# Six norm stages of a two-block transformer: turning rows by a product with a diagonal instead of scaling and then transposing

## The chip, the cores and the metric

The kernel is one program on one core of a Trainium2 chip. The metric is the device time of one execution in microseconds (us); lower is better. The time before is a median of 4292.33 us over 3 runs (4291.05 to 4294.51). About 0.2% of it, some 8.6 us, is what a measurement of this kernel can tell from no change.

## The reference

Two transformer blocks on 512 latent tokens ("lat") and 256 context tokens ("ctx") of width 1024. The first has three mixers (pooling, differential attention, a bidirectional linear recurrence) and a mixture of experts; the second has two layers, one with a convolution and a gated recurrence, one with latent attention, each followed by a feed-forward part. What matters here is the norm that precedes each of these parts:

```
def rms_norm(x, g):
    xf = x.astype(jnp.float32)
    y = xf * lax.rsqrt(jnp.mean(xf * xf, axis=-1, keepdims=True) + NORM_EPS)
    return (y * g.astype(jnp.float32)).astype(x.dtype)

def modulate(x, g, shift, scale):
    return rms_norm(x, g) * (1 + scale) + shift
```

Tokens of the two kinds have their own shift and scale. All is float32.

## The kernel before

The program is a row of stages. Each stage is one block in which the five engines run their own instruction lists, tied by semaphores, with a barrier of all engines at its end (helper `stage`, L48; the barrier's records stand on L57). So whatever a stage takes stands in full on the path of the whole, and nothing of the next stage's engine work begins before it ends. Only a weight tile that `bring_ahead` (L155) has asked for before the stage lands beside it.

Rows of tokens are 128x1024 tiles (partition = token, free = feature). The products that follow need them turned: partition = feature, in 8 chunks of 128 features, free = token. `normed` (L436) does norm, modulation and turning, and is called six times:

- stage 1 (`first_normed`, L837): 6 tiles, 2 ctx and 4 lat
- stage 2 (L872): 4 lat tiles before the experts; the only one whose result is one float32 tensor `hT`
- stages 3, 4 and 5 (L2104 for both layers, L2128 in layer 0): 6 tiles each
- stage 6 (L2128 in layer 1): 4 lat tiles

Except in stage 2 the result is stored as two parts, because the products on L302 work on fp32r operands in three products of parts: `parts[0]` is the result rounded to fp32r ("leading"), `parts[1]` is what rounding left over ("rest"), so that their sum is the float32 value.

How the work goes in one such stage:

- ScalarE squares each tile and sums it along the row (L459), one square after the other; VectorE divides by 1024 and adds epsilon for all tiles at once (L479); ScalarE takes the root (L461, its function table is loaded ahead of it); VectorE takes the reciprocal (L481).
- For each tile: ScalarE multiplies the rows with 1/root into `xn` (L466, two buffers); TensorE turns the 8 chunks with the transpose instruction against the identity `m.ident` (L517), four to a PSUM bank, four banks in turn; a semaphore is raised after each half tile (4 chunks).
- For each half tile VectorE reads the four chunks out of PSUM, each in an instruction of its own over 128 tokens because gain and shift are values per feature, that is per partition (L499), into `whole` (two half tiles); ScalarE rounds the half (`round_tile`, L452); VectorE subtracts to get the rest (`rest_of`, L487). VectorE's list holds the rest of the half tile before the previous one ahead of the four reads, since it frees the half of `whole` that they write.
- In stage 2 the reads on L499 write `hT` straight away and L452 and L487 don't run.

The identity product elsewhere that resembles the new one is in `gate_rows` (L412): `nc.tensor.matmul(..., wide, m.ident)`, L423, an ordinary float32 product of a 128x128 tile with a 128x128 matrix.

Of the kernel before, what the change touches and what calls it, by code (L numbers as in the profile page):

```python
# [6 lines left out]
ALU = mybir.AluOpType  # L7
# [4 lines left out]
P = 128  # L12
# [423 lines left out]
def normed(nc, m, tiles, hT, affine):  # L436
# [4 lines left out]
    kinds = sorted(affine)  # L441
    n = len(tiles)
    with ExitStack() as ctx:
        b = Memory()
        b.xn, b.sq, b.whole, b.ss, b.root, b.rstd, b.gain = buffers(nc, ctx, xn=[2, D], sq=[2, D], whole=[2, 4, P], ss=[n], root=[n], rstd=[n], gain=[len(kinds), KD])
        with stage(nc, squared=1, summed=1, rooted=1, inverse=1, scaled=1, turned=1, read=1, rounded=1, rest=1, chain=1) as (
                block, squared_sem, summed_sem, rooted_sem, inverse_sem, scaled_sem, turned_sem, read_sem, rounded_sem, rest_sem, chain_sem):
            def round_tile(act, i):

                for h in range(2):  # L450
                    act.wait_ge(read_sem, 2 * i + h + 1)
                    nc.scalar.copy(parts[0][:, 4 * h:4 * h + 4, tiles[i][1]:tiles[i][1] + P], b.whole[:, h, :, :]).then_inc(rounded_sem, 1)  # L452

            @block.scalar
            def _(act):
                for i, (x, t0, k) in enumerate(tiles):
                    if i >= 2:
                        act.wait_ge(squared_sem, i - 1)
                    nc.scalar.activation(b.sq[:, i % 2, :], x, ACT.Square, accum_out=b.ss[:, i:i + 1]).then_inc(squared_sem, 1)  # L459
                act.wait_ge(summed_sem, 1)  # L460
                nc.scalar.activation(b.root[:, :], b.ss[:, :], ACT.Sqrt).then_inc(rooted_sem, 1)  # L461
                act.wait_ge(inverse_sem, 1)
                for i in range(n):
                    if i >= 2:
                        act.wait_ge(turned_sem, 2 * (i - 1))
                    nc.scalar.activation(b.xn[:, i % 2, :], tiles[i][0], ACT.Copy, scale=b.rstd[:, i:i + 1]).then_inc(scaled_sem, 1)  # L466
                    if parts and i:
                        round_tile(act, i - 1)
                if parts:
                    round_tile(act, n - 1)  # L470

            @block.vector
            def _(dve):
# [29 lines left out]
                if parts:  # L503
                    rest_of(2 * n - 2)
                    rest_of(2 * n - 1)
# [2383 lines left out]
```

## Time and profile before

| | us |
|---|---|
| median of 3 runs | 4292.33 |
| lowest, highest | 4291.05, 4294.51 |
| the profiled execution | 4297.7 |
| its span, first to last instruction | 4295.5 |
| TensorE busy (82% of the span) | 3530.9 |
| TensorE weight loads busy (64%) | 2753.6 |
| VectorE busy (40%) | 1717.3 |
| ScalarE busy (21%) | 882.8 |
| mean granted TensorE clock | 0.908 |

The profile's page gives, for the whole span, busy time by engine, a coarse timeline, the chain of work that ended last and the costliest groups of instructions by line. The trace behind it can be asked for a timeline (instructions in order of time, neighbours merged), for stretches (busy time of each engine between two times, with the granted clock) and for groups of instructions by line and shape. Of one group the mean duration is of a single instruction; neighbouring instructions of one engine overlap a little, so that a run of them is shorter than the sum of their durations. A granted clock of 1.00 stands for 2.4 GHz, 0.50 for 1.2 GHz.

### The profile page before, as it was taken

What the parts mean: (1) busy time and instruction counts of PE and PEld (TensorE: products, weight loads), DVE (VectorE), ACT (ScalarE), POOL (GpSimd) and SP (SyncE); (2) the same over time, 40 slices, a digit from 0 to 9 for tenths busy, and PEclk for the clock granted to TensorE, in tenths of its full rate; (3) what the DMA queues carried; (4) which work ended last, traced back from release to release, by engine and by line L of the source; (5) the groups of instructions that cost most, each with busy time, mean ns of one, the idle gap of its engine ahead of it and who ended that gap; (6) DMA issues with size and microseconds to landing.
All of it is one profiled execution on the core that took longest, in us unless ns stands there. A gap on an engine that the chain in (4) does not pass through costs nothing. (4 is left out here: it accounts for less than half of the span.)

```text
span 4295.5 us, 68450 instructions
## 1 busy us (share of the span) xinstructions
PE 3530.9 (82%) x29742; PEld 2753.6 (64%) x29742; DVE 1717.3 (40%) x3137; ACT 882.8 (21%) x1426; POOL 57.0 (1%) x74
## 2 busy tenths in 40 slices
PE   4979988588986577773989976799989868979997
PEld 2858986556646333332746846688878765567887
DVE  3655544562134000004545265544420254245643
ACT  2135430042101011112011151211100112323221
POOL 0000000000000100000000000000000000000000
PEclk7979998789987799996999988899999879989998
DMA  5130006203331899993521101244421010013322
GB/s 210 60 124 4 4 10 188 84 11 111 114 112 52 326 422 424 422 422 101 155 87 54 50 2 40 68 116 112 118 91 54 0 47 25 1 35 90 97 79 79
DMA packets 379410, 494.18 MB, mean 115 GB/s; under 512 B 15994, under 2 KB 325787, under 8 KB 370436
## 3 DMA queue, kind: packets, MB, share of 16 engines
q1 hardware_dynamic: 369588, 456.12, 30.7%
q0 software_dynamic: 4432, 25.70, 1.5%
q10 hardware_dynamic: 5120, 8.39, 0.5%
q8 instruction: 215, 3.52, 0.3%
q14 instruction: 55, 0.45, 0.0%
HBM read 458.70 MB, written 31.47 MB: 114 GB/s over the span
## 5 line engine op out<-in xcount | busy, mean ns | idle before, releaser
L302 PE MATMUL banks<-leading,w_rest 128*128 128x512 f32 (+2 forms) x1920 | 699.1, 364 | 63.9 <-DVE w_rest L262 63.9
L302 PE MATMUL banks<-rest,w_leading 128*128 128x512 f32 (+2 forms) x1920 | 691.7, 360 | 0.0
L302 PE MATMUL banks<-leading,w_leading 128*128 128x512 f32 (+2 forms) x1920 | 691.1, 360 | 0.0
L302 PEld LDWEIGHTS banks<-leading,w_rest 128*128 128x128 f32 (+1 forms) x1920 | 365.1, 190 | 125.2 <-DVE w_rest L262 48.0
L302 PE MATMUL banks<-w_rest,leading 128*128 128x256 f32 (+3 forms) x1332 | 394.1, 296 | 57.0 <-DVE w_rest L262 57.0
L262 DVE TENSOR_TENSOR w_rest<-land,w_leading 128x1024 fp32r<-128x1024 f32 (+3 forms) x296 | 280.0, 988 | 357.5 <-ACT w_leading L256 357.5
L302 PEld LDWEIGHTS banks<-leading,w_leading 128*128 128x128 f32 (+1 forms) x1920 | 364.7, 190 | 59.5
L302 PEld LDWEIGHTS banks<-rest,w_leading 128*128 128x128 f32 (+1 forms) x1920 | 365.1, 190 | 57.3
L256 ACT CAST w_leading<-land 128x1024 fp32r<-128x1024 f32 (+3 forms) x296 | 239.7, 857 | 741.0 <-DMA land<-in_w_in 311.9
L302 PE MATMUL banks<-w_leading,rest 128*128 128x256 f32 (+3 forms) x1332 | 390.2, 293 | 0.0
L302 PE MATMUL banks<-w_leading,leading 128*128 128x256 f32 (+3 forms) x1332 | 389.7, 293 | 0.0
L302 PEld LDWEIGHTS banks<-w_rest,leading 128*128 128x128 f32 x1332 | 261.8, 197 | 62.3 <-DVE w_rest L262 54.0
L302 PEld LDWEIGHTS banks<-w_leading,rest 128*128 128x128 f32 x1332 | 261.7, 196 | 1.4
L302 PEld LDWEIGHTS banks<-w_leading,leading 128*128 128x128 f32 x1332 | 261.5, 196 | 1.4
L302 PE MATMUL banks<-w,fT 128*128 128x256 f32 x1056 | 230.0, 381 | 11.9 <-DMA w<-in_ffn_down 11.9
L302 PEld LDWEIGHTS banks<-w,fT 128*128 128x128 f32 x1056 | 201.9, 191 | 39.8 <-DMA w<-in_ffn_down 12.0
L1725 DVE TENSOR_TENSOR t<-banks,gate_rows 128x256 f32<-128x256 f32 x96 | 40.7, 424 | 349.4 <-PE banks L302 349.4
L1929 PE MATMUL banks<-wu,xT 128*64 128x256 f32 x1024 | 130.8, 413 | 59.9 <-DMA wu<-in_w_exp_up 59.9
L517 PE MATMUL banks<-ident,xn 128*128 128x128 f32 x256 | 59.7, 418 | 137.3 <-ACT xn L466 137.1
L348 DVE COPY side_rows<-banks 128x128 f32<-128x128 f32 x128 | 37.2, 291 | 312.7 <-PE banks L311 312.5
L1929 PEld LDWEIGHTS banks<-wu,xT 128*64 128x64 f32 x1024 | 76.9, 148 | 113.6 <-DMA wu<-in_w_exp_up 74.0
L1984 DVE TENSOR_TENSOR h<-sg,banks 128x256 f32<-128x256 f32 x32 | 13.5, 421 | 337.4 <-PE banks L1929 337.4
(532 smaller groups left out, 4803.3 us busy)
## 6 DMA issues: line engine op xcount, KB each, us to landing
wg<-in_w_exp_gate SPq DMA_DIRECT2D x32, 2048.0 KB, 28.4
wu<-in_w_exp_up SPq DMA_DIRECT2D x32, 2048.0 KB, 28.4
wd<-in_w_exp_down SPq DMA_DIRECT2D x32, 2048.0 KB, 27.9
ws<-in_ada_w SPq DMA_DIRECT2D x96, 512.0 KB, 3.9
land<-in_w_in SPq DMA_DIRECT2D x41, 1024.0 KB, 5.6
land<-in_ffn_up SPq DMA_DIRECT2D x44, 512.0 KB, 5.4
land<-in_ffn_up SPq DMA_DIRECT2D x88, 256.0 KB, 3.4
ws<-in_w_ada SPq DMA_DIRECT2D x32, 512.0 KB, 4.1
```

Of the source, the lines that this page charges most:

```text
L256: nc.scalar.copy(leading[s % 2][:, k0:k1, 0:n], slots[s % wslots][:, k0:k1, 0:n]).then_inc(rounded_sem, 1)
L262: nc.vector.tensor_tensor(rest[s % 2][:, k0:k1, 0:n], slots[s % wslots][:, k0:k1, 0:n], leading[s % 2][:, k0:k1, 0:n].bitcast(F32), ALU.su ...
L302: mm = nc.tensor.matmul(bank_of(r, kind, at), lhsT, rhs, start=(k == 0 and q == 0), stop=(k == kt - 1 and q == len(each) - 1))
L348: nc.vector.tensor_copy(side_rows[t % 2][:, :], m.ps[:, 6 + t % 2, 0:P]).then_inc(side_copied_sem, 1)
L517: mm = nc.tensor.transpose(m.ps[:, q % 4, j * P:(j + 1) * P], b.xn[:, i % 2, f * P:(f + 1) * P], m.ident)
L1725: chain(nc.vector.tensor_tensor(b.t[:, turn[0], 0:width], out, g[:, c], ALU.mult))
L1929: mm = nc.tensor.matmul(m.ps[SLOTS * c:SLOTS * (c + 1), bank, half(u)], b.xT[:, k, S], w[u][:, k, half(c)], start=(k == 0), stop=(k == KD ...
L1984: nc.vector.tensor_tensor(b.h[:, :], b.sg[:, :], m.ps[:, 3, half(u)], ALU.mult).then_inc(h_new_sem, 1)
```

## The change

Within `normed` alone:

- The rows are no longer scaled by 1/root into `xn`. VectorE writes for each tile a 128x128 diagonal `diag` = identity times 1/root (a value per token). TensorE multiplies each 128x128 chunk of the unscaled tile, as the stationary operand, with that diagonal in an ordinary float32 product: the result is the chunk turned and scaled at once. `xn` and the transposes are gone.
- The results go by feature chunk: a unit is one kind of token (ctx, then lat) and one chunk of 128 features, 256 or 512 tokens wide, in one PSUM bank; eight banks in turn. There are 16 units for 6 tiles, 8 for 4.
- Gain and shift are applied to a whole unit in one instruction, by ScalarE for chunks 2, 5 and 7, by VectorE for the other five. `whole` has four buffers of one unit; ScalarE rounds each unit (after the unit that follows has been read, where that one is its own), VectorE makes the rest two units behind.
- The root is taken for each kind by itself: the ctx root stands on ScalarE behind the first lat square, the lat root behind the last. VectorE makes the ctx diagonals, then waits for the lat squares and makes the lat diagonals, and only then reads units; TensorE begins the ctx units when the ctx diagonals are there.
- TensorE waits, from the ninth unit on, until the unit eight before has been read, by whichever engine reads it.

```diff
--- before.py
+++ after.py
@@ -439,83 +439,133 @@
 
     parts = hT if isinstance(hT, list) else None
     kinds = sorted(affine)
+    of_kind = [[i for i, tile in enumerate(tiles) if tile[2] == k] for k in kinds]
+    units = [(g, f) for g in range(len(kinds)) for f in range(KD)]
     n = len(tiles)
     with ExitStack() as ctx:
         b = Memory()
-        b.xn, b.sq, b.whole, b.ss, b.root, b.rstd, b.gain = buffers(nc, ctx, xn=[2, D], sq=[2, D], whole=[2, 4, P], ss=[n], root=[n], rstd=[n], gain=[len(kinds), KD])
-        with stage(nc, squared=1, summed=1, rooted=1, inverse=1, scaled=1, turned=1, read=1, rounded=1, rest=1, chain=1) as (
-                block, squared_sem, summed_sem, rooted_sem, inverse_sem, scaled_sem, turned_sem, read_sem, rounded_sem, rest_sem, chain_sem):
-            def round_tile(act, i):
-
-                for h in range(2):
-                    act.wait_ge(read_sem, 2 * i + h + 1)
-                    nc.scalar.copy(parts[0][:, 4 * h:4 * h + 4, tiles[i][1]:tiles[i][1] + P], b.whole[:, h, :, :]).then_inc(rounded_sem, 1)
+        b.sq, b.diag, b.whole, b.ss, b.root, b.rstd, b.gain = buffers(nc, ctx, sq=[2, D], diag=[n, P], whole=[4, 512], ss=[n], root=[n], rstd=[n], gain=[len(kinds), KD])
+
+        def by_scalar(u):
+
+            return units[u][1] % 8 in (2, 5, 7)
+
+        def span(u):
+
+            own = of_kind[units[u][0]]
+            return slice(tiles[own[0]][1], tiles[own[0]][1] + P * len(own))
+
+        def bank(u):
+
+            return m.ps[:, u % 8, 0:P * len(of_kind[units[u][0]])]
+
+        def whole(u):
+
+            if parts is None:
+                return hT[:, units[u][1], span(u)]
+            return b.whole[:, u % 4, 0:P * len(of_kind[units[u][0]])]
+
+        def scalars_of(u):
+
+            g, f = units[u]
+            return b.gain[:, g, f:f + 1], affine[kinds[g]][2][:, f:f + 1]
+
+        taken_by = {True: [], False: []}
+        for u in range(len(units)):
+            taken_by[by_scalar(u)].append(u)
+
+        with stage(nc, squared=1, summed=1, rooted=1, gained=1, spread=1, turned=1, read_act=1, read_dve=1, rounded=1, rest=1, chain=1) as (
+                block, squared_sem, summed_sem, rooted_sem, gained_sem, spread_sem, turned_sem, read_act_sem, read_dve_sem, rounded_sem, rest_sem, chain_sem):
+            def wait_read(eng, u):
+
+                if by_scalar(u):
+                    eng.wait_ge(read_act_sem, taken_by[True].index(u) + 1)
+                else:
+                    eng.wait_ge(read_dve_sem, taken_by[False].index(u) + 1)
 
             @block.scalar
             def _(act):
-                for i, (x, t0, k) in enumerate(tiles):
-                    if i >= 2:
-                        act.wait_ge(squared_sem, i - 1)
-                    nc.scalar.activation(b.sq[:, i % 2, :], x, ACT.Square, accum_out=b.ss[:, i:i + 1]).then_inc(squared_sem, 1)
-                act.wait_ge(summed_sem, 1)
-                nc.scalar.activation(b.root[:, :], b.ss[:, :], ACT.Sqrt).then_inc(rooted_sem, 1)
-                act.wait_ge(inverse_sem, 1)
-                for i in range(n):
-                    if i >= 2:
-                        act.wait_ge(turned_sem, 2 * (i - 1))
-                    nc.scalar.activation(b.xn[:, i % 2, :], tiles[i][0], ACT.Copy, scale=b.rstd[:, i:i + 1]).then_inc(scaled_sem, 1)
-                    if parts and i:
-                        round_tile(act, i - 1)
+                done = 0
+
+                def root(g):
+                    own = of_kind[g]
+                    act.wait_ge(summed_sem, g + 1)
+                    nc.scalar.activation(b.root[:, own[0]:own[-1] + 1], b.ss[:, own[0]:own[-1] + 1], ACT.Sqrt).then_inc(rooted_sem, 1)
+
+                for g, own in enumerate(of_kind):
+                    for at, i in enumerate(own):
+                        if done >= 2:
+                            act.wait_ge(squared_sem, done - 1)
+                        nc.scalar.activation(b.sq[:, done % 2, :], tiles[i][0], ACT.Square, accum_out=b.ss[:, i:i + 1]).then_inc(squared_sem, 1)
+                        done += 1
+                        if at == 0 and g:
+                            root(g - 1)
+                root(len(kinds) - 1)
+
+                def round_unit(u):
+
+                    wait_read(act, u)
+                    nc.scalar.copy(parts[0][:, units[u][1], span(u)], whole(u)).then_inc(rounded_sem, 1)
+
+                act.wait_ge(gained_sem, len(kinds))
+                for u in range(len(units)):
+                    if by_scalar(u):
+                        act.wait_ge(turned_sem, u + 1)
+                        if parts and u >= 4:
+                            act.wait_ge(rest_sem, u - 3)
+                        gain, shift = scalars_of(u)
+                        nc.scalar.activation(whole(u), bank(u), ACT.Identity, bias=shift, scale=gain).then_inc(read_act_sem, 1)
+                    if parts and u:
+                        round_unit(u - 1)
                 if parts:
-                    round_tile(act, n - 1)
+                    round_unit(len(units) - 1)
 
             @block.vector
             def _(dve):
                 chain = Chain(dve, chain_sem)
                 for i, k in enumerate(kinds):
                     g, scale, shift = affine[k]
-                    chain(nc.vector.scalar_tensor_tensor(b.gain[:, i, :], scale, 1.0, g, ALU.add, ALU.mult))
-                dve.wait_ge(squared_sem, n)
-                nc.vector.tensor_scalar(b.ss[:, :], b.ss[:, :], 1.0 / D, EPS, ALU.mult, ALU.add).then_inc(summed_sem, 1)
-                dve.wait_ge(rooted_sem, 1)
-                nc.vector.reciprocal(b.rstd[:, :], b.root[:, :]).then_inc(inverse_sem, 1)
-
-                def rest_of(q):
-
-                    f, t0 = 4 * (q % 2), tiles[q // 2][1]
-                    dve.wait_ge(rounded_sem, q + 1)
-                    nc.vector.tensor_tensor(parts[1][:, f:f + 4, t0:t0 + P], b.whole[:, q % 2, :, :],
-                                            parts[0][:, f:f + 4, t0:t0 + P].bitcast(F32), ALU.subtract).then_inc(rest_sem, 1)
-
-                for i, (x, t0, k) in enumerate(tiles):
-                    shift = affine[k][2]
-                    for h in range(2):
-                        dve.wait_ge(turned_sem, 2 * i + h + 1)
-                        if parts and i:
-                            rest_of(2 * i + h - 2)
-                            dve.wait_ge(rest_sem, 2 * i + h - 1)
-                        for j in range(4):
-                            f = 4 * h + j
-                            last = nc.vector.tensor_scalar(
-                                b.whole[:, h, j, :] if parts else hT[:, f, t0:t0 + P], m.ps[:, (2 * i + h) % 4, j * P:(j + 1) * P],
-                                b.gain[:, kinds.index(k), f:f + 1], shift[:, f:f + 1], ALU.mult, ALU.add)
-                        last.then_inc(read_sem, 1)
+                    nc.vector.scalar_tensor_tensor(b.gain[:, i, :], scale, 1.0, g, ALU.add, ALU.mult).then_inc(gained_sem, 1)
+                dve.wait_ge(gained_sem, len(kinds))
+                done = 0
+                for g, own in enumerate(of_kind):
+                    T = slice(own[0], own[-1] + 1)
+                    done += len(own)
+                    dve.wait_ge(squared_sem, done)
+                    nc.vector.tensor_scalar(b.ss[:, T], b.ss[:, T], 1.0 / D, EPS, ALU.mult, ALU.add).then_inc(summed_sem, 1)
+                    dve.wait_ge(rooted_sem, g + 1)
+                    chain(nc.vector.reciprocal(b.rstd[:, T], b.root[:, T]))
+                    for i in own:
+                        nc.vector.tensor_scalar(b.diag[:, i, :], m.ident, b.rstd[:, i:i + 1], None, ALU.mult).then_inc(spread_sem, 1)
+
+                def rest_of(u):
+
+                    dve.wait_ge(rounded_sem, u + 1)
+                    nc.vector.tensor_tensor(parts[1][:, units[u][1], span(u)], whole(u), parts[0][:, units[u][1], span(u)].bitcast(F32), ALU.subtract).then_inc(rest_sem, 1)
+
+                for u in range(len(units)):
+                    if not by_scalar(u):
+                        dve.wait_ge(turned_sem, u + 1)
+                        if parts and u >= 4:
+                            dve.wait_ge(rest_sem, u - 3)
+                        gain, shift = scalars_of(u)
+                        nc.vector.tensor_scalar(whole(u), bank(u), gain, shift, ALU.mult, ALU.add).then_inc(read_dve_sem, 1)
+                    if parts and u >= 2:
+                        rest_of(u - 2)
                 if parts:
-                    rest_of(2 * n - 2)
-                    rest_of(2 * n - 1)
+                    rest_of(len(units) - 2)
+                    rest_of(len(units) - 1)
 
             @block.tensor
             def _(pe):
-                for i in range(n):
-                    pe.wait_ge(scaled_sem, i + 1)
-                    for h in range(2):
-                        q = 2 * i + h
-                        if q >= 4:
-                            pe.wait_ge(read_sem, q - 3)
-                        for j in range(4):
-                            f = 4 * h + j
-                            mm = nc.tensor.transpose(m.ps[:, q % 4, j * P:(j + 1) * P], b.xn[:, i % 2, f * P:(f + 1) * P], m.ident)
-                        mm.then_inc(turned_sem, 1)
+                for u, (g, f) in enumerate(units):
+                    if f == 0:
+                        pe.wait_ge(spread_sem, sum(len(own) for own in of_kind[0:g + 1]))
+                    if u >= 8:
+                        wait_read(pe, u - 8)
+                    for at, i in enumerate(of_kind[g]):
+                        mm = nc.tensor.matmul(bank(u)[:, at * P:(at + 1) * P], tiles[i][0][:, f * P:(f + 1) * P], b.diag[:, i, :], start=True, stop=True)
+                    mm.then_inc(turned_sem, 1)
 
 
 def head_norms(nc, m, xs, width, eps, out_scale=None):
```

## Rows read from the trace of the kernel before

**Rows 1.** The six stages as stretches; columns as the first line names them.

```profile
core 0: us, PE busy (x) PEld busy (x) DVE busy (x) ACT busy (x) POOL busy (x), PEclk, DMA share, GB/s
43.26:77.77 34.51, 11.55 (x48) 9.55 (x48) 24.27 (x64) 21.66 (x32) 0.00 (x0) 0.50 0.00 0
1327.35:1346.02 18.67, 6.87 (x32) 6.12 (x32) 10.81 (x35) 10.24 (x14) 0.00 (x0) 0.67 0.00 0
...
3846.86:3871.26 24.40, 7.61 (x32) 6.41 (x32) 16.22 (x43) 15.00 (x22) 0.00 (x0) 0.55 0.00 0
sum 180.09, PE 59.69 PEld 50.02 DVE 124.11 ACT 110.58 POOL 0.00; mean PE 9.95 PEld 8.34 DVE 20.68 ACT 18.43 POOL 0.00
```

**Rows 2.** Timeline of stage 1 up to its first transposes: start, duration, instruction [idle before].

```profile
49.42 0.19 ACT L459 ACTIVATION_READ_ACCUMULATOR sq<-x_first 128x1 f32 x1
49.62 1.28 ACT L461 ACT_TABLE_LOAD   x1
49.71 0.17 DVE L479 TENSOR_SCALAR ss<-ss 128x6 f32<-128x6 f32 x1 [6.05 <-ACT sq L459]
50.92 0.21 ACT L461 ACTIVATE root<-ss 128x6 f32<-128x6 f32 x1
51.16 0.19 DVE L481 RECIPROCAL rstd<-root 128x6 f32<-128x6 f32 x1 [1.28 <-ACT root L461]
```

**Rows 3.** Timeline of stage 1, a tile in its steady part, and its end.

```profile
57.02 1.37 DVE L499 TENSOR_SCALAR whole<-banks,gain,mod 128x128 f32<-128x128 f32 x4
58.14 1.57 PEld L517 LDWEIGHTS banks<-ident,xn 128*128 128x128 f32 x8 [2.28 <-ACT xn L466]
...
76.31 1.46 DVE L487 TENSOR_TENSOR rest<-whole,leading 128x512 fp32r<-128x512 f32 x2
```

**Rows 4.** ScalarE's timeline ahead of and in stage 4, which has no table load.

```profile
2589.85 1.28 ACT L533 ACT_TABLE_LOAD   x1 [19.24 <-PEq L57]
...
2708.17 1.04 ACT L459 ACTIVATE sq<-x_rows 128x1024 f32<-128x1024 f32 x1
...
2709.61 0.21 ACT L461 ACTIVATE root<-ss 128x6 f32<-128x6 f32 x1 [0.32 <-DVE ss L479]
```

**Rows 5.** Timeline of weight loads of ordinary float32 128x128 products, on L423 and L638.

```profile
1264.14 3.49 PEld L423 LDWEIGHTS banks<-ident,wide 128*128 128x128 f32 x16 [11.02 <-DVE wide L429]
...
922.46 1.41 PEld L638 LDWEIGHTS banks<-v,aT 128*128 128x128 f32 x12 [0.33 <-issue]
```

**Rows 6.** Granted clock in stretches of back-to-back products (L2046, then L1773); columns as in Rows 1.

```profile
1346.60:1351.50 4.90, 4.82 (x24) 4.60 (x24) 2.39 (x2) 0.00 (x0) 0.00 (x0) 0.57 0.17 68
1351.50:1353.00 1.50, 1.09 (x8) 0.86 (x8) 0.47 (x2) 0.00 (x0) 0.00 (x0) 1.00 0.73 298
1363.90:1377.50 13.60, 13.59 (x64) 13.60 (x64) 0.00 (x0) 0.00 (x0) 0.00 (x0) 0.50 0.00 0
```

**Rows 7.** Groups by shape: count | busy us, mean ns of one | idle before.

```profile
L499 DVE TENSOR_SCALAR whole<-banks,gain,mod 128x128 f32<-128x128 f32 x224 | 76.1, 404 | 13.6 <-PE banks L517 11.9
L487 DVE TENSOR_TENSOR rest<-whole,leading 128x512 fp32r<-128x512 f32 x56 | 38.3, 684 | 0.4
L1726 DVE TENSOR_TENSOR x_rows<-x_rows,t 128x256 f32<-128x256 f32 x80 | 34.0, 425 | 2.8
L987 DVE TENSOR_SCALAR rw<-pad,cols 128x512 f32<-128x512 f32 x15 | 7.3, 487 | 0.5
L397 DVE TENSOR_SCALAR mixT<-banks,cols 128x128 f32<-128x128 f32 x24 | 6.3, 341 | 1.0 <-PE banks L386 1.0
L397 DVE TENSOR_SCALAR brT<-banks,subln 128x512 f32<-128x512 f32 x4 | 3.0, 752 | 2.0 <-PE banks L386 1.7
L987 DVE TENSOR_SCALAR rw<-pad,cols 128x256 f32<-128x256 f32 x10 | 3.5, 354 | 0.4
L452 ACT CAST leading<-whole 128x512 fp32r<-128x512 f32 x56 | 34.7, 619 | 55.8 <-DVE whole L499 55.8
L2406 ACT ACTIVATE gi<-banks,cols 8x512 f32<-8x512 f32 x1 | 0.7, 680 | 5.1 <-PE banks L302 5.1
```

## The prediction

> **What bounds the kernel now.** I read first what a norm stage is to the whole: a block with a barrier behind it, so the time of the kernel is a sum over stages, and only the length of these six counts. The stretches come next [rows 1]: together the six last 180.09 us, 4.2% of the span. In stage 1 (34.51 us) VectorE is busy 24.27, ScalarE 21.66, TensorE 11.55; no DMA runs. The timeline tells the order. Up to the end of the reciprocal the stage is a serial chain of 8.09 us (43.26 to 51.35) [rows 2]. From the first read on it is VectorE that ends last: per half tile four reads in 1.37 us and one rest of 0.68, with hand-overs some 2.0 us, and TensorE's 8 transposes of a tile, 1.57 us of weight loads, come after 2.28 us of idle time [rows 3]. Stages 3 and 5 repeat stage 1; stage 4 is 1.0 us shorter, since no table is loaded in it; stage 6 is the same with 4 tiles (24.40 us), stage 2 (18.67) has no rounding and no rest. The granted clock is mostly low in them (0.50 in stage 1) [rows 1], as TensorE waits.
>
> **The change part by part**, for a stage of 6 tiles first, times from its first square.
>
> *Up to the diagonals.* Six squares and the last sum are done at 6.35 us (49.42 + 0.19 - 43.26) [rows 2]. The table load now stands among them, with the same price: 1.28, with its gap 1.4. The ctx root (0.21, gap 0.1) is added. Before, the division (L479) lay beside the table load; now that of the lat tiles lies bare, 0.17 + 0.05. Then the lat root 0.21 and the reciprocal 0.19 with gaps: 6.35 + 1.4 + 0.3 + 0.22 + 0.24 + 0.2, or 8.7. A diagonal is a 128-wide read of SBUF with one pointer operand: from 354 ns at 256 and 487 at 512 [rows 7], 0.29, of which about 0.08 overlaps the next (four reads of 404 ns take 1.37 [rows 3, 7]), so 0.21. Bounds: 0.17 (nearly all fixed cost, as L479) and 0.40 (as the read on L499). Four of them: VectorE is free at 9.6, against a first read at 53.74 - 43.26, or 10.5, before. The `xn` multiplications, 1.14 each on ScalarE, go.
>
> *VectorE after that.* A 512-wide read of a bank with one pointer takes 752 ns, a second pointer adds 404 - 341, so 0.81, less the overlap 0.73; bounds 0.61 (a read without pointers would be that) and 1.29 (as four small ones). At 256 wide, between 404 ns at 128 and 0.81 at 512: 0.54, or 0.46. A rest is 0.68, or 0.60; at 256 wide 425 ns, or 0.34 [rows 7]. VectorE has five reads and eight rests of each kind: ctx 5 x 0.46 + 8 x 0.34 = 5.0, lat 5 x 0.73 + 8 x 0.60 = 8.45, together 13.45. From 9.6 on: 23.05. Before, its like was 12 x 2.0.
>
> *ScalarE.* Three reads and eight roundings of a kind: 0.68 and 0.62 at 512 [rows 7], 0.47 and 0.40 estimated from the same groups at 256, less 0.1 overlap: 3 x (0.58 + 0.37) + 8 x (0.52 + 0.30) = 9.4, so it hides under VectorE's 13.45. The root among the squares would cost more if Square needed another table. It does not: in stage 4 squares and root follow a root load of long before without a new one [rows 4].
>
> *TensorE.* Sixteen weight-load records last 3.49 us at the low clock: the 8 products of L423, two records each, so 0.436 a product; at the high clock 12 records of L638 last 1.41, so 0.235 [rows 5]. A transpose was 1.57 / 8 = 0.196 [rows 3]. So TensorE's work more than doubles at equal clock. The ctx diagonals are there at 5.5 (three squares 3.2, load 1.4, root, reciprocal, two diagonals 0.9). From then on eight banks are free and 16 ctx products run beside the squares: until 12.5 at the low clock. The 32 lat products take 7.5 at the high clock, 14.0 at the low. The clock decides: back-to-back products on L2046 were granted 0.57 in 4.9 us and 1.00 in the stretch behind it; on L1773 others kept 0.50 throughout 13.6 us [rows 6]. I take that it rises during the ctx units, as on L2046, whose products move 128 columns as the new ones do and are also of one short block. Then TensorE is done at 18 to 20, ahead of VectorE, and the stage ends at 23.1: 34.51 - 23.1 = 11.4 saved. Stage 4 moves both ends alike, so 4 x 11.4 = 45.6.
>
> The Trainium skill (TensorE: Matmul & The Clock Gate, Part 4: PE-mode transpose) says that transposes don't count as activity for the clock. Here the trace disagrees: those of L2046 were followed by 1.00 [rows 6]. By that rule the old stage could never warm and the new one would; the sum would be the same.
>
> *Stage 6.* The reciprocal ends at 6.0; with four diagonals (0.9) the first product starts at 7.0. Nothing runs ahead of it, so TensorE bounds: 8 to 12 products at 0.436, the rest at 0.235, or 9.1 to 9.9: done at 16.0 to 16.9. The last unit is ScalarE's: hand-over 0.3, read 0.68, round 0.62, rest 0.68 and gaps, 2.5. Laid out unit by unit the waits for late first units push VectorE's 8.45 us of work, begun at 9.1 and broken by them, to about 20.0. Saved 4.4.
>
> *Stage 2.* The same to 16.0 to 16.9, then hand-over and one read, 1.1: about 17.7. Saved 1.0; here VectorE had only ten us of reads, and halving them is nearly all given to TensorE.
>
> Sum: 45.6 + 4.4 + 1.0 = 51.0. The profiled execution took 4297.7, so 4246.7; the median of the runs lies 5.4 below it, so I forecast 4241 for the median. What follows a stage is late next in no case: the weight tile ahead of each landed long before, and the blocks behind start with casts from it.
>
> **The rivals.**
>
> *The clock stays low.* For: stage 1 was granted 0.50 [rows 1], L1773 too. Against: L2046. Then a 6-tile stage is bound by TensorE: 5.5 + 48 x 0.436 + 2.6 = 29.0, stage 6 7.0 + 14.0 + 2.5 = 23.5, stage 2 7.0 + 14.0 + 1.1 = 22.1, longer than before by 3.4. Saved 4 x 5.5 + 0.9 - 3.4 = 19.5: 4273.
>
> *Hand-overs.* A unit passes bank, read, round and rest over two engines. If the rest, two units behind, still finds the rounding unfinished, VectorE waits. For: the last two rests of stage 1 take 1.46 instead of 1.28 [rows 3]. Against: 0.4 us of waits before 56 rests [rows 7]. At 0.3 a unit: 16 x 0.3 x 4 + 8 x 0.3 = 21.6 lost, 4263.
>
> *Slower: the product costs four transposes.* An ordinary float32 product may take four passes where a transpose takes one. With a low clock the savings over all stages are 131.2 - 256 c for a product of c us (131.2 being the old stages less the heads and tails above), so the change loses from c = 0.51 on. Four times 0.196 is 0.784: 131.2 - 200.7 = -69.5, 4362. Against: 0.436 measured for the same shape [rows 5]. The Trainium skill (TensorE: Matmul & The Clock Gate, Terms) gives the transpose mode as four times faster for float32; by it the sum would be that of this rival; the rows show 2.2 times.
>
> **How the numbers follow.** Forecast 0.80, low clock 0.10, hand-overs 0.07, costly product 0.03 (0.02 of it past the turning point by more than can be told, 0.01 near it). About 0.2%, 8.6 us, can be told from no change. Faster 0.97, same 0.01, slower 0.02. Range: at the low end reads of 0.61 and diagonals of 0.17 save about 7 us more: 4234. At the high end it takes in the hand-overs, dearer reads and a clock that rises late in some stages: 4264. The low-clock case and beyond stay out, with some of the ends: 2 in 10.
>
> **What would show it.** In a 6-tile stage: VectorE without idle time from about 9.6 us to the end, reads of 128x512 near 0.81 us, a stage of 23 us; TensorE's first product near 5.5, 96 records, granted clock 1.00 by the lat units; ScalarE's table load behind the third square and no second one. Stage 2 nearly as long as before. Wrong would be: idle time of VectorE that TensorE's banks end (clock or price of a product), or that ScalarE's roundings end (hand-overs), or a second table load.

## The result and the profile after

The changed kernel takes 4246.02 us (median of 4 runs, 4245.46 to 4247.24) against 4293.42 (4 runs): a ratio of 0.989, 95% interval 0.9873 to 0.9907, 47.4 us less. Run again beside 13 runs of the kernel before (4288.84 to 4301.02, median 4295.38) it took 4245.1, ratio 0.9883 (0.9867 to 0.99), 50.3 us less. The forecast was 4241, within 4234 to 4264. Of the ten runs of products_twice, an experiment below, one took 13327.7 us at a mean granted clock of 0.53 where the other nine took 4292.4 to 4296.4; the ratios leave it out.

The six stages in the profile after, as stretches from barrier to barrier (columns as the first line names them), to be set against [rows 1]. The three lines behind the first are parts of stage 1:

```profile
core 0: us, PE busy (x) PEld busy (x) DVE busy (x) ACT busy (x) POOL busy (x), PEclk, DMA share, GB/s
43.18:66.42 23.24, 13.19 (x96) 13.00 (x96) 15.73 (x38) 18.62 (x37) 0.00 (x0) 0.78 0.00 1
48.76:51.76 3.00, 3.00 (x14) 3.00 (x15) 0.35 (x2) 2.55 (x7) 0.00 (x0) 0.50 0.00 0
51.76:54.53 2.77, 2.77 (x20) 2.77 (x20) 2.66 (x9) 1.31 (x4) 0.00 (x0) 0.70 0.00 0
54.53:61.95 7.42, 7.42 (x67) 7.23 (x65) 7.42 (x17) 6.38 (x15) 0.00 (x0) 1.00 0.00 1
1319.67:1336.71 17.04, 8.98 (x64) 8.79 (x64) 5.44 (x12) 8.09 (x13) 0.00 (x0) 0.80 0.00 1
1973.97:1997.52 23.55, 13.74 (x96) 13.55 (x96) 15.73 (x38) 18.61 (x37) 0.00 (x0) 0.72 0.00 1
2681.60:2703.42 21.82, 13.91 (x96) 13.71 (x96) 15.73 (x38) 17.22 (x36) 0.00 (x0) 0.81 0.00 1
3376.85:3400.09 23.24, 13.74 (x96) 13.55 (x96) 15.73 (x38) 18.61 (x37) 0.00 (x0) 0.74 0.00 1
3801.44:3820.46 19.02, 8.84 (x64) 8.64 (x64) 10.07 (x20) 12.32 (x21) 0.00 (x0) 0.82 0.00 1
```

VectorE's busy time in stage 1 fell from 24.27 to 15.73 us. TensorE's 96 records (two to a product) were granted 0.50, then 0.70, then 1.00 in those three parts of stage 1. Now the timeline of stage 1, where [rows 2, 3] of before show the serial head and the half tiles:

```profile
46.49 1.28 ACT L493 ACT_TABLE_LOAD   x1
47.78 0.20 ACT L493 ACTIVATE root<-ss 128x2 f32<-128x2 f32 x1
...
48.76 5.85 PEld L567 LDWEIGHTS banks<-diag,xc_first 128*128 128x128 f32 x32 [14.41 <-DVE diag L539]
...
51.13 0.17 DVE L535 TENSOR_SCALAR ss<-ss 128x4 f32<-128x4 f32 x1 [2.43 <-ACT sq L499]
51.34 0.21 ACT L493 ACTIVATE root<-ss 128x4 f32<-128x4 f32 x1 [0.24 <-DVE ss L535]
51.58 0.18 DVE L537 RECIPROCAL rstd<-root 128x4 f32<-128x4 f32 x1 [0.27 <-ACT root L493]
51.79 0.88 DVE L539 TENSOR_SCALAR diag<-ident,rstd 128x128 f32<-128x128 f32 x4
52.58 0.99 DVE L552 TENSOR_SCALAR whole<-banks,gain,mod 128x256 f32<-128x256 f32 x2
...
54.53 7.23 PEld L567 LDWEIGHTS banks<-diag,x_first 128*128 128x128 f32 x64
...
62.98 0.80 DVE L552 TENSOR_SCALAR whole<-banks,gain,mod 128x512 f32<-128x512 f32 x1
...
63.71 2.48 DVE L544 TENSOR_TENSOR rest<-whole,leading 128x512 fp32r<-128x512 f32 x4
```

The table load stands among the squares and no second one follows. From 52.58 on no VectorE line has idle time beside it, to the end of its last rest at 66.19. In stages 4 and 5 it is the same, and in stage 3 VectorE waits 0.4 us in all, for a rounding. TensorE runs without a break from 48.76 to 61.95 and ends 4.2 us ahead of it. The groups by shape (count | busy us, mean ns | idle before) carry the terms of the sum:

```profile
L552 DVE TENSOR_SCALAR whole<-banks,gain,mod 128x512 f32<-128x512 f32 x25 | 20.1, 805 | 3.1 <-PE banks L567 3.1
L552 DVE TENSOR_SCALAR whole<-banks,gain,mod 128x256 f32<-128x256 f32 x20 | 10.4, 538 | 0.0
L544 DVE TENSOR_TENSOR rest<-whole,leading 128x512 fp32r<-128x512 f32 x40 | 25.7, 682 | 0.0
L544 DVE TENSOR_TENSOR rest<-whole,leading 128x256 fp32r<-128x256 f32 x32 | 12.7, 418 | 0.6 <-ACT leading L508 0.4
L539 DVE TENSOR_SCALAR diag<-ident,rstd 128x128 f32<-128x128 f32 x32 | 7.2, 283 | 0.4
L552 DVE TENSOR_SCALAR hT<-banks,gain,mod 128x512 f32<-128x512 f32 x5 | 4.0, 810 | 4.9 <-PE banks L567 4.9
L517 ACT ACTIVATE whole<-banks,mod,gain 128x512 f32<-128x512 f32 x15 | 11.6, 776 | 1.7 <-PE banks L567 1.1
```

The 3.1 us that VectorE waits for banks at its 512-wide reads all lie in stage 6, 2.2 of them ahead of its first read there.

### The profile page after: what moved, and what is told of

Its sections match the earlier page's. It is cut to its first block and busy times, and to the rows that moved or that the text cites. A ratio compares the mean times of both kernels' runs of the same rounds, so it can differ in the third digit from the quotient of the medians.

```text
span 4244.0 us, 68832 instructions
## 1 busy us (share of the span) xinstructions
PE 3545.1 (84%) x29998; PEld 2774.8 (65%) x29998; DVE 1671.6 (39%) x2987; ACT 865.2 (20%) x1444; POOL 56.9 (1%) x74
## 5 line engine op out<-in xcount | busy, mean ns | idle before, releaser
L1994 PE MATMUL banks<-wd,hT 128*64 128x512 f32 x512 | 116.9, 598 | 30.4 <-ACT hT L2018 30.4
```

The lines of the kernel that those rows point to most:

```text
L1994: mm = nc.tensor.matmul(m.ps[SLOTS * n:SLOTS * (n + 1), 5 + u, :], b.hT[:, j, SLOTS * c:SLOTS * (c + 1)], wd[u][:, k, n * 512:(n + 1) * 51 ...
```

## The experiments

All but the first are edits of the changed kernel, each run beside the kernel before. Since an edit moves a stage by one to ten microseconds and the total scatters by a few, the length of the stages in each trace, barrier to barrier, is what is compared. "Others" is the span less the six.

| run | stage 1 | 2 | 3 | 4 | 5 | 6 | sum | others | median of 4 |
|---|---|---|---|---|---|---|---|---|---|
| before | 34.81 | 19.28 | 34.80 | 33.80 | 34.80 | 24.70 | 182.2 | 4113.3 | 4293 to 4295 |
| after | 23.24 | 17.04 | 23.55 | 21.82 | 23.24 | 19.02 | 127.9 | 4116.0 | 4246.0 |
| as_changed | 23.24 | 16.95 | 23.55 | 21.82 | 23.24 | 20.03 | 128.8 | 4116.5 | 4245.1 |
| vector_reads_all | 26.59 | 16.90 | 26.58 | 25.17 | 26.59 | 21.99 | 143.8 | 4110.3 | 4258.4 |
| products_twice | 32.77 | 24.14 | 32.39 | 31.66 | 31.59 | 27.21 | 179.8 | 4114.7 | 4294.7 |
| transposed_by_chunk | 28.05 | 17.53 | 28.05 | 26.63 | 28.05 | 20.81 | 149.1 | 4112.2 | 4264.0 |
| narrow_reads | 26.79 | 16.96 | 27.08 | 25.37 | 26.78 | 21.69 | 144.7 | 4114.1 | 4262.0 |
| roots_at_end | 24.64 | 16.96 | 24.68 | 23.22 | 24.69 | 20.33 | 134.5 | 4115.8 | 4252.7 |
| warmed | 23.24 | 15.48 | 23.54 | 21.83 | 23.24 | 17.59 | 124.9 | 4114.4 | 4240.1 |
| four_and_four | 22.01 | 18.04 | 22.01 | 20.71 | 22.27 | 19.99 | 125.0 | 4113.1 | 4242.5 |
| pool_rests | 22.98 | 18.10 | 22.97 | 21.24 | 22.69 | 19.98 | 128.0 | 4111.6 | 4240.6 |
| warmed_four | 22.01 | 15.48 | 22.02 | 20.60 | 22.02 | 17.32 | 119.4 | 4111.4 | 4230.1 |

(The median of products_twice is of its 10 runs.)

**The changed kernel again.** The six stages gave 54.3 us in the first pair of traces, the total 47.4: is some of it given back behind them?

> The changed kernel once more, as the base of all that follows. If what the norm stages gain is what counts, the six stages together last 126 us again (180.1 before), and the median lies near 4246. The other stages were 2.8 us longer in the one trace of the changed kernel than in the one of before, in pieces of one or two microseconds of both signs. Theory A: that is scatter from one execution to the next, so the same pieces differ again by as much between two executions of the very same kernel. Theory B: the change gives time back in the stages behind, so the same pieces (+1.4 in the products of the recurrence's inputs, +1.9 and +0.9 in the layer with the convolution) are there again with the same sign.

Measured: 4245.1 us, stages 128.8. "Others" lies between 4110.3 and 4116.5 over all twelve traces, with that of before (4113.3) in the middle, though no edit touches them. Part of that is scatter between two executions of this one kernel: the block with the recurrence's scan differs by 1.6 us, one in the second layer's attention by 1.5. But the three pieces that theory B named came back with the sign they had: +0.8, +1.9 and +0.3 us against before. The 1.9 us lie in one block, shown here for before, as_changed and vector_reads_all, the next experiment, in this order:

```profile
2497.31:2589.78 92.47, 82.56 (x432) 56.19 (x432) 61.89 (x184) 41.86 (x100) 0.00 (x0) 0.94 0.01 3
...
2472.11:2566.46 94.35, 85.30 (x432) 56.96 (x432) 61.90 (x184) 41.83 (x100) 0.00 (x0) 0.91 0.01 3
...
2476.39:2568.83 92.44, 82.56 (x432) 56.24 (x432) 61.88 (x184) 41.83 (x100) 0.00 (x0) 0.94 0.01 3
```

In the twelve traces this block lasts either 92.4 to 92.5 us or 94.3 to 94.4, the shorter at a mean granted clock of 0.94, the longer at 0.91. It was the longer in both traces of the changed kernel and in six of the edited ones, the shorter in before and in three edited ones. So neither theory holds as it stands: the piece is no scatter from one execution to the next, and it is no loss that the change always brings. "Others" of the eleven traces behind the change average 4113.6 us, against 4113.3 in the only trace of before, and a give-back of some 2 us can't be told from that. Of the 6.9 us between 54.3 and 47.4 only 2.7 lie in "others"; the rest comes from setting traces beside medians, since the profiled execution of before (4297.7) lay 4.3 us above its median.

**Does VectorE bound the stages of 6 tiles?**

```diff
-            return units[u][1] % 8 in (2, 5, 7)
+            return False
```

> VectorE reads all units out of PSUM, none is read by ScalarE. Theory A (VectorE bounds the stages of 6 tiles): it gets three more reads of each kind, 3 x 0.73 + 3 x 0.46 = 3.6 us, and each of those four stages is longer by that, stage 2 hardly at all (TensorE bounds it, 8 x 0.73 fit under its 9 us), stage 6 by about 1.5: total 4246 + 16 = 4262. Theory B (TensorE or the hand-overs bound them): no stage is longer by more than 1 us, 4246 to 4250.

Measured: 4258.4 us (ratio 0.9917, 0.99 to 0.9933). Stages 1, 3, 4 and 5 are longer by 3.0 to 3.4 us, stage 6 by 2.0 to 3.0, stage 2 by nothing. Theory A, with 3.6 in each a little too dear. VectorE's reads show waits for TensorE of 4.0 and 2.7 us, and all of them lie in stages 6 and 2; in the four stages of 6 tiles VectorE has no idle time behind its first read:

```profile
L552 DVE TENSOR_SCALAR whole<-banks,gain,mod 128x512 f32<-128x512 f32 x40 | 32.1, 803 | 4.0 <-PE banks L567 4.0
L552 DVE TENSOR_SCALAR hT<-banks,gain,mod 128x512 f32<-128x512 f32 x8 | 6.5, 810 | 3.2 <-PE banks L567 2.7
```

**What do the wide reads give?**

```diff
-                        nc.vector.tensor_scalar(whole(u), bank(u), gain, shift, ALU.mult, ALU.add).then_inc(read_dve_sem, 1)
+                        for at in range(len(of_kind[units[u][0]])):
+                            T = slice(at * P, (at + 1) * P)
+                            last = nc.vector.tensor_scalar(whole(u)[:, T], bank(u)[:, T], gain, shift, ALU.mult, ALU.add)
+                        last.then_inc(read_dve_sem, 1)
```

> VectorE reads its units in pieces of 128 tokens again (four or two instructions a unit), all else stays as changed. Theory A (VectorE bounds the stages of 6 tiles, and its time goes with the number of instructions as on L499 of before): 5 x (1.29 - 0.73) = 2.8 us for lat and 5 x (0.64 - 0.46) = 0.9 for ctx more in each of those four, about 1.5 in stage 6, at most 0.5 in stage 2: 4245 + 16 = 4261. If the width of the reads were not what pays, under 4250.

Measured: 4262.0 us (0.9928, 0.9911 to 0.9944). The four stages are longer by 3.5 to 3.6 us, 3.7 expected. The small reads last 401 ns, as on L499 of before [rows 7]; stage 2, where TensorE ends last, does not notice them:

```profile
L554 DVE TENSOR_SCALAR whole<-banks,gain,mod 128x128 f32<-128x128 f32 x140 | 48.1, 401 | 3.0 <-PE banks L570 3.0
```

**What does the diagonal give?** The transposes come back, the rest of the change stays. The core of the edit:

```diff
-                        nc.vector.tensor_scalar(b.diag[:, i, :], m.ident, b.rstd[:, i:i + 1], None, ALU.mult).then_inc(spread_sem, 1)
+                        nc.scalar.activation(b.xn[:, slot(i), :], tiles[i][0], ACT.Copy, scale=b.rstd[:, i:i + 1]).then_inc(spread_sem, 1)
...
-                        mm = nc.tensor.matmul(bank(u)[:, at * P:(at + 1) * P], tiles[i][0][:, f * P:(f + 1) * P], b.diag[:, i, :], start=True, stop=True)
+                        mm = nc.tensor.transpose(bank(u)[:, at * P:(at + 1) * P], b.xn[:, slot(i), f * P:(f + 1) * P], m.ident)
```

> The diagonal is undone, all else of the change stays: ScalarE multiplies the rows with 1/root into xn again (four buffers, where the squares are written too), TensorE turns them with the transpose instruction, still by chunk, with wide reads and both engines reading. Theory A (the diagonal pays because it takes the row multiplications off the serial head and off ScalarE): ScalarE has 6 x 1.05 us more, of which the four lat ones (4.2) and the two ctx ones (2.1) lie ahead of the lat units, while the diagonals (0.9) go: stages of 6 tiles 4 to 5.5 us longer than now, stages 2 and 6 about 1 us longer, since the transposes cost TensorE half: total about 4246 + 20 = 4266. Theory B (what pays is the wide reads alone): within 5 us of 4246, and stages 2 and 6 shorter.

Measured: 4264.0 us (0.9928, 0.9911 to 0.9945). Stages 1, 3, 4 and 5 are longer by 4.5 to 4.8 us. The timeline of stage 1 shows where:

```profile
47.60 2.17 ACT L504 ACTIVATE xn<-xc_first,rstd 128x1024 f32<-128x1024 f32 x2
...
52.53 4.26 ACT L504 ACTIVATE xn<-x_first,rstd 128x1024 f32<-128x1024 f32 x4 [0.24 <-DVE rstd L551]
56.70 0.39 ACT L522 CAST leading<-whole 128x256 fp32r<-128x256 f32 x1
...
57.13 0.43 DVE L556 TENSOR_TENSOR rest<-whole,leading 128x256 fp32r<-128x256 f32 x1 [3.75 <-ACT leading L522]
```

ScalarE multiplies rows for 4.26 us, its first rounding comes after that, and VectorE waits 3.75 us for it; it had also begun 1.2 us later. That is theory A, and it is why the product pays although TensorE works longer for it: in stage 2 TensorE is busy 6.38 us with transposes and 8.98 with products, and still the stage is 0.5 us longer with transposes. The 4.8 us hold for this order of ScalarE's list, in which the four lat rows are multiplied ahead of the first ctx rounding. An order with the ctx roundings first might wait less; no run tried it.

**The turning point of the slower rival.** Each product twice, so that its price doubles:

```diff
+                        nc.tensor.matmul(bank(u)[:, at * P:(at + 1) * P], tiles[i][0][:, f * P:(f + 1) * P], b.diag[:, i, :], start=True, stop=True)
```

> Each product with a diagonal is issued twice into the same place, so that the price of a product doubles and nothing else changes. The slower rival of the prediction put the turning point at 0.51 us a product. Theory A (TensorE is hidden in the stages of 6 tiles and bounds those of 4): a product now costs 0.87 at the low and 0.46 at the high clock, TensorE ends last everywhere: stages of 6 tiles about 32 us (23 now), stage 6 about 26.5, stage 2 about 25: total near 4298, no gain left against before. If the clock stayed low all the way, more than 4340.

Measured: 4294.7 us, ratio 0.9996 (0.9986 to 1.0006): nothing that can be told is left of the gain, and 2.4 us of it in the stages (179.8 against 182.2). VectorE now waits 33.5 us for banks at its 512-wide reads (3.1 in the changed kernel):

```profile
L552 DVE TENSOR_SCALAR whole<-banks,gain,mod 128x512 f32<-128x512 f32 x25 | 20.3, 810 | 33.5 <-PE banks L568 33.5
L544 DVE TENSOR_TENSOR rest<-whole,leading 128x512 fp32r<-128x512 f32 x40 | 26.1, 684 | 5.5 <-ACT leading L508 5.5
```

TensorE's busy time in the six stages is 129.4 us here for 256 places, so 0.505 us each. The prediction's formula, 131.2 less 256 times the price, leaves 1.9 us at that price and nothing at 0.51. What the low clock all the way would cost is not shown by this, since the clock rose here too (0.80 to 0.89 over the stages). It shows only that a price of this size ends the gain.

**What is the head start of the ctx units worth?**

```diff
-                        if at == 0 and g:
-                            root(g - 1)
-                root(len(kinds) - 1)
+                for g in range(len(kinds)):
+                    root(g)
```

> Both roots are taken behind the last square, so that no ctx product runs beside the squares; TensorE begins at about 8.9 us of a stage of 6 tiles, not at 5.5. Theory A (the head start hides TensorE's stretch at the low clock): the low stretch of some 5 us now lies in front of the reads, VectorE waits for units, and each such stage is 1.5 to 2.5 us longer; stages 2 and 6 the same: about 4253. Theory B (the head start is worth nothing, as VectorE alone sets the end): within 1 us of 4246, perhaps shorter, because a root less interrupts the squares.

Measured: 4252.7 us (0.9903, 0.9887 to 0.992), the four stages longer by 1.1 to 1.4 us, a little less than expected. Times have to be taken from the barrier here, which stands at 42.56 in this trace and at 43.18 in that of the changed kernel. TensorE's first product comes 8.7 us behind it instead of 5.6. VectorE's first read comes at 10.0 instead of 9.4, because the ctx root and its diagonals now stand in the same chain as the lat ones, and then VectorE waits 0.8 us for TensorE (0.27 and 0.53). These two, 0.6 and 0.8, are the 1.4 us of stage 1, so the head start of the products alone is worth 0.8:

```profile
51.25 4.85 PEld L566 LDWEIGHTS banks<-diag,xc_first 128*128 128x128 f32 x30 [18.66 <-DVE diag L538]
...
53.36 0.54 DVE L551 TENSOR_SCALAR whole<-banks,gain,mod 128x256 f32<-128x256 f32 x1 [0.27 <-PE banks L566]
...
54.77 0.55 DVE L551 TENSOR_SCALAR whole<-banks,gain,mod 128x256 f32<-128x256 f32 x1 [0.53 <-PE banks L566]
```

**Does the clock set stages 2 and 6?** In the traces of the changed kernel TensorE begins them at 0.50.

```diff
             def _(pe):
+                for _ in range(24 if n == 4 else 18):
+                    nc.tensor.matmul(m.ps[:, 7, 0:P], m.ident, m.ident, start=True, stop=True)
```

> TensorE runs 18 or (with 4 tiles) 24 products of the identity with itself into a bank not yet in use while ScalarE squares; their result is never read. Theory A (in the stages of 4 tiles TensorE ends last and begins at the low clock): its first 12 or so products take 0.235 us instead of 0.436, so stages 2 and 6 are about 2 us shorter each and the stages of 6 tiles the same within 0.5: about 4242. Theory B (the clock does not follow what ran just before, or the extra products delay the first real one): no stage shorter, 4246 or more.

Measured: 4240.1 us (0.9873, 0.9857 to 0.989). Stage 2 is 1.5 us shorter than in as_changed, stage 6 is 2.4 (1.4 against the first trace), those of 6 tiles are the same to 0.01. The half of theory B that feared for the first real product came true in stage 3, where it begins 7.1 us behind the barrier instead of 5.6, but VectorE's first read did not come later. The granted clock in both stages of 4 tiles was 1.00, against 0.80 and 0.72 in as_changed:

```profile
1318.43:1333.91 15.48, 13.01 (x112) 12.65 (x112) 5.44 (x12) 8.09 (x13) 0.00 (x0) 1.00 0.01 2
...
3798.13:3815.72 17.59, 13.01 (x112) 12.66 (x112) 10.06 (x20) 12.33 (x21) 0.00 (x0) 1.00 0.00 1
```

**Has ScalarE room?**

```diff
-            return units[u][1] % 8 in (2, 5, 7)
+            return units[u][1] % 8 in (1, 3, 5, 7)
```

> ScalarE reads four of the eight chunks (1, 3, 5, 7), VectorE four. Theory A (VectorE bounds the stages of 6 tiles and ScalarE has room under it, 9.4 us of work against 13.45): VectorE loses a read of each kind, 0.73 + 0.46 = 1.2 us a stage, ScalarE gains 0.95 and stays below: four times -1.2, stage 6 -0.5, stage 2 the same: about 4240. Theory B (ScalarE's roundings then come late and VectorE waits for them): the four stages keep their length or grow.

Measured: 4242.5 us (0.9882, 0.9865 to 0.9898). Stages 1 and 3 to 5 are shorter by 1.0 to 1.5 us: theory A. Stage 6 gained nothing that can be told (19.99 against 20.03 and 19.02; 0.5 was expected). Stage 2 came out 1.1 us longer at a granted clock of 0.72, against 0.80 in as_changed. The edit is hardly why: in pool_rests below, whose edit leaves stage 2 alone, it took 18.10 us at the same 0.72. Three us after its first product the clock was still at the low level, where that of the first trace had risen; the second line of each pair is that stretch:

```profile
1326.50:1329.50 3.00, 2.95 (x14) 2.96 (x15) 0.81 (x1) 0.00 (x0) 0.00 (x0) 0.50 0.02 5
1329.50:1332.50 3.00, 3.00 (x18) 3.00 (x18) 0.42 (x1) 0.78 (x1) 0.00 (x0) 0.59 0.00 0
```

(four_and_four, stage 2; below the first trace of the changed kernel, stage 2)

```profile
1326.70:1329.70 3.00, 3.00 (x14) 3.00 (x15) 0.81 (x1) 0.00 (x0) 0.00 (x0) 0.50 0.02 5
1329.70:1332.70 3.00, 3.00 (x27) 3.00 (x27) 1.38 (x2) 0.78 (x1) 0.00 (x0) 0.95 0.00 0
```

**GpSimd for two of eight rests.** The subtraction for chunks 1 and 4 moves to GpSimd, with a semaphore of its own:

```diff
+            @block.gpsimd
+            def _(pool):
+                if parts:
+                    for u in rest_by[True]:
+                        pool.wait_ge(rounded_sem, u + 1)
+                        nc.gpsimd.tensor_tensor(parts[1][:, units[u][1], span(u)], whole(u), parts[0][:, units[u][1], span(u)].bitcast(F32), ALU.subtract).then_inc(rest_pool_sem, 1)
```

> GpSimd, idle in these stages so far, makes the rest of chunks 1 and 4; otherwise as changed. Theory A (VectorE bounds the stages of 6 tiles): it loses 2 x 0.60 + 2 x 0.34 = 1.9 us of each, if GpSimd's subtraction is done before its buffer is wanted two or three units later: four times -1.9, stage 6 about -0.5: 4237. Theory B (GpSimd's subtraction is slow, or slows VectorE, which reads and writes SBUF beside it): VectorE's reads wait for the buffer or last longer, and the stages keep their length or grow. No trace so far shows the price of such an operation.

Measured: 4240.6 us (0.9873, 0.9856 to 0.9889), but the stages together are hardly shorter (128.0 against 128.8): those of 6 tiles by 0.3 to 0.6 each, where 1.9 was expected, and stage 2 longer by 1.1 with its late clock. Most of the lower total is "others" (4111.6 against 4116.5), which the edit does not touch. The price did stand in a trace: before has eight operations of two 128x512 tiles on GpSimd (L1481), 1270 ns each. VectorE's own rests became longer beside GpSimd's:

```profile
L576 POOL TENSOR_TENSOR rest<-whole,leading 128x512 fp32r<-128x512 f32 x10 | 12.7, 1272 | 434.4 <-ACT leading L518 434.4
...
L556 DVE TENSOR_TENSOR rest<-whole,leading 128x512 fp32r<-128x512 f32 x30 | 22.0, 771 | 0.0
L556 DVE TENSOR_TENSOR rest<-whole,leading 128x256 fp32r<-128x256 f32 x24 | 11.6, 496 | 1.5 <-ACT leading L518 1.3
```

771 ns against 681 in as_changed, 496 against 417. The 20 rests of 128x512 that overlap no operation of GpSimd take 681 as in as_changed; of the 10 that do, five take 679 to 683 and five 1184 to 1343. So theory B for most of it.

**Both edits that helped.**

> Both of the last two edits: TensorE busy ahead of its first unit, and four reads of eight on ScalarE. The two touch different stages (those bound by TensorE, those bound by VectorE), so their gains should add: stages together 128.8 - 3.5 - 4.8 = 120.5 us, total about 4237.

Measured: 4230.1 us (4227.24 to 4232.88), ratio to before 0.9846 (0.9829 to 0.9862), stages 119.4. They add: 3.9 us less in the stages of 4 tiles (warmed) and 4.9 less in those of 6 (four_and_four) leave about 120 of 128.8; 119.4 were measured. This version beats both kernels, the changed one by about 15 us; of those 9.4 lie in the stages, and the rest in parts that scatter.

## Why the prediction was right, point by point

- *Up to the diagonals.* VectorE was to be free at 9.6 us; its first read began at 52.58 - 43.24, or 9.3. Four diagonals took 0.88 (0.9 said), one 283 ns (0.29 said).
- *VectorE after that.* 805 ns for a 512-wide read (0.81 said), 538 for 256 (0.54), rests 682 and 418 (684, 425). It ended at 66.19, or 22.95 us after the first square; 23.05 was said. The step that carried the sum was the price of a read: the one row with one pointer operand (a value per partition, here the gain), and for the second pointer the difference of two small rows.
- *ScalarE.* Its reads were priced by a row with one pointer, 0.68; they took 776 to 779 ns with two. The Trainium skill (ScalarE: Activation LUTs, What ACT_TABLE_LOAD costs) gives 186 ns + 0.833 ns a column and about 93 ns for each pointer operand. For 512 columns and two pointers that is an estimate of 799 ns, 3% above what was measured and closer than my row. ScalarE hid under VectorE all the same: four_and_four shows room for one more read of each kind.
- *TensorE.* 5.5 us for its first product (48.76 - 43.24, or 5.5), clock 1.00 by the lat units, end at 18.7 (18 to 20 said). Sixteen ctx products were said to run beside the squares until 12.5. Only five or six did (14 records, or seven products, in the first 3.00 us, and the last square ended 2.35 us after the first product); the others ran beside the root, the diagonals and VectorE's first reads, until 11.4. In stage 1 roots_at_end puts 0.8 us on that head start and 0.6 on the earlier ctx root and diagonals.
- *Stages 2 and 6* were mis-sized. Stage 6 was to last 20.0 us and lasted 18.7 from first square to last rest in the first trace, 19.7 in the second; stage 2 was to last 17.7 and lasted 16.75 and 16.66. In stage 6 VectorE's first read came at 9.1 as said, and its work behind that took 8.7 us without the waits (8.45 said). The waits for late first units were put at 2.4 us (20.0 - 9.1 - 8.45). They were 0.97 in the first trace and 1.99 in the second, where TensorE took 9.85 us for its products and not 8.84. The stage is longer by the same 1.0 us, so these waits do stand in full in its length; the term was too large. First trace above, second below:

```profile
3811.98 0.81 DVE L552 TENSOR_SCALAR whole<-banks,gain,mod 128x512 f32<-128x512 f32 x1 [0.59 <-PE banks L567]
...
3813.76 0.81 DVE L552 TENSOR_SCALAR whole<-banks,gain,mod 128x512 f32<-128x512 f32 x1 [0.38 <-PE banks L567]
```

```profile
3812.76 0.81 DVE L552 TENSOR_SCALAR whole<-banks,gain,mod 128x512 f32<-128x512 f32 x1 [0.90 <-PE banks L567]
...
3815.25 0.81 DVE L552 TENSOR_SCALAR whole<-banks,gain,mod 128x512 f32<-128x512 f32 x1 [1.09 <-PE banks L567]
```

In stage 2 the products took 8.98 us (9.1 to 9.9 said), and hand-over and last read 0.8 (1.1 said).
- *The sum* said 51.0; from first square to last result the stages gave 54.0 (180.1 less 126.1), and 53.1 in the second trace. Of the 3.0 us above the forecast 0.8 lie in the stages of 6 tiles (0.6 of them in stage 4, which was to gain the same 11.4 and gained 12.0), 0.9 in stage 2 and 1.3 in stage 6. The totals gave 47.4 and 50.3, less than the stages did, in part because the other blocks took 2.7 and 3.2 us more than in the trace of before. These two errors have opposite signs. That the total came within 5 us of 4241 is in that part luck; that each stage of 6 tiles came within 0.6 us is not.
- *The rivals.* The clock rose in every one of the 6-tile stages. Why it did there and on L2046, whose records are transposes, and not in the 13.6 us on L1773 [rows 6], no run shows: the choice between the two rows came true, it was not derived. VectorE waited for roundings 0.4 us in all, so hand-overs cost next to nothing. A product took 0.43 us at the low clock (seven in 3.00 us), as the row of L423 said (0.436), and 0.23 at the high (32 in 7.31). With the price doubled the gain was gone at 0.505 us a product, where the prediction's formula put 0.51.

What the parts are worth in a stage of 6 tiles, each undone alone in stage 1: the diagonal 4.8 us, the wide reads 3.55, ScalarE's share of the reads 3.35, the early ctx root 1.4. They sum to 13.1 where the whole change gives 11.6: undone alone, a part shows its price with all the others in place, and that of the diagonal also holds the order of ScalarE's list.

## What to carry to other kernels

Where a per-row factor is applied ahead of a transpose, try folding it into the transpose as a product with a diagonal. Here it paid although a product cost TensorE 2.2 times a transpose (0.436 against 0.196 us at the low clock), since the engine that scaled the rows stood on the path and TensorE waited; work out first at which price of a product the gain is gone. Lay results out so that one instruction covers as many columns as share the same scalars. And a block that is short and begins cold has its clock to pay for: give TensorE idle products while it waits, but only where TensorE ends last.

## What the hardware showed that was not expected

- The same code, stage 6 of the changed kernel, took 19.02 us in one execution and 20.03 in another. In the stretch from about 3 to 6 us behind the first product the granted clock was 1.00 in one and 0.64 in the other. So the moment at which the clock rose differed between two executions of one program, and was worth 1 us of this stage. The first trace is the odd one: five edited kernels that issue each product once and begin the stage cold (vector_reads_all, narrow_reads, roots_at_end, four_and_four, pool_rests) had 0.70 to 0.73 over stage 6, as_changed 0.72, and only the first trace 0.82.
- A subtraction of two 128x512 SBUF tiles on GpSimd took 1272 ns, and the 30 like ones that VectorE kept went from 681 to 771 ns on average. The Trainium skill (SBUF — State Buffer, Terms) says that the two engines take a shared pair of ports in turn and the loser waits for the whole instruction; the trace agrees: each of the five long VectorE rests (1184 to 1343 ns) began while a GpSimd operation ran and ended 0.55 us behind that operation's end, and rests that overlapped none took 681.
